# A two-layer sequence trunk: its long convolution as half-length transforms over even and odd tokens, and a new order of the first mixer

## The reference, cut to what matters

```python
def hyena_mix(u, k_hat, conv_w, conv_b, skip):
    parts = jnp.split(short_conv3(u, conv_w, conv_b), 3, axis=-1)
    z = fft_long_conv(parts[0] * parts[1], k_hat[:, 0], skip[0])
    return z * parts[2]

def fft_long_conv(z, k_hat, skip):               # k_hat = rfft of a learned filter of 2L taps
    z_hat = jnp.fft.rfft(z, n=2 * L, axis=1)
    y = jnp.fft.irfft(z_hat * k_hat, n=2 * L, axis=1)[:, :L]
    return y + z * skip

# GLA, per head and chunk of 64 tokens, forward and backward in time
att = tril(q_in @ k_in.T);  o = att @ v + q_in @ state_before;  state = decay * state + k_st.T @ v
y = concat([hyena(hy), rms_norm(o_f + o_b) * silu(g)]) @ w_out
```

## Time and profile before

| | |
|---|---|
| median of three runs | 1725.1 us |
| the profiled execution, its own time | 1726.82 us |
| its span on the core | 1725.0 us |
| TensorE busy | 1688.2 us, 98% |
| VectorE busy | 1154.5 us, 67% |
| ScalarE busy | 683.7 us, 40% |
| GpSimd busy | 72.3 us, 4% |
| bytes moved | 249.73 MB, mean 145 GB/s |

### The profile page before, as it was taken

The page is one execution under the profiler, slowest core; times in us unless marked ns, Lnnn a source line. Parts: engine busy times, 40 slices in busy tenths (PEclk is TensorE's granted clock), DMA queues, the critical chain, the costliest instruction groups (busy, mean ns, idle before and its releaser), DMA issues. The chain is left out here.

```text
span 1725.0 us, 24359 instructions
## 1 busy us (share of the span) xinstructions
PE 1688.2 (98%) x9608; PEld 1438.4 (83%) x9608; DVE 1154.5 (67%) x1791; ACT 683.7 (40%) x1058; POOL 72.3 (4%) x60
## 2 busy tenths in 40 slices
PE   7999999999999999999999999999999999989997
PEld 4788888889778679888888889888888888889997
DVE  5477949877385767677733366879466787765556
ACT  4443232225353326532222237322232267664443
POOL 1000000011000011000000020000000110100001
PEclk9999999999999999999999999999999999989998
DMA  9565546632332011555322233554466342245653
GB/s 333 222 207 173 169 157 212 211 92 74 112 116 83 26 58 73 197 187 182 112 97 94 84 139 101 197 175 154 162 216 204 92 144 77 75 142 161 205 165 110
DMA packets 86375, 249.73 MB, mean 145 GB/s; under 512 B 8740, under 2 KB 24261, under 8 KB 86262
## 3 DMA queue, kind: packets, MB, share of 16 engines
q1 hardware_dynamic: 85592, 246.25, 43.1%
q0 software_dynamic: 448, 1.51, 0.2%
q10 hardware_dynamic: 222, 0.43, 0.1%
HBM read 247.10 MB, written 1.05 MB: 144 GB/s over the span
## 5 line engine op out<-in xcount | busy, mean ns | idle before, releaser
L1872 PE MATMUL bank<-a_hi,w_hi 128*128 128x512 f32 (+1 forms) x1528 | 556.9, 364 | 7.6 <-DVE yt L1696 2.8
L1873 PE MATMUL bank<-a_hi,w_lo 128*128 128x512 f32 (+1 forms) x1528 | 555.1, 363 | 0.0
L1874 PE MATMUL bank<-a_lo,w_hi 128*128 128x512 f32 (+1 forms) x1528 | 555.1, 363 | 0.0
L1154 DVE TENSOR_TENSOR w_lo<-raw,w_hi 128x1024 fp32r<-128x1024 f32 (+1 forms) x338 | 381.6, 1129 | 177.0 <-ACT w_hi L775 170.0
L775 ACT CAST w_hi<-raw 128x1024 fp32r<-128x1024 f32 (+1 forms) x338 | 320.2, 953 | 162.5 <-DMA raw<-in_dram 155.2
L1872 PEld LDWEIGHTS bank<-a_hi,w_hi 128*128 128x128 f32 x1528 | 289.2, 189 | 55.3 <-issue 7.9
L1874 PEld LDWEIGHTS bank<-a_lo,w_hi 128*128 128x128 f32 x1528 | 289.2, 189 | 45.0
L1873 PEld LDWEIGHTS bank<-a_hi,w_lo 128*128 128x128 f32 x1528 | 289.2, 189 | 44.7
L1172 DVE SCALAR_TENSOR_TENSOR acc<-ada,scol,acc 128x1024 f32<-128x1024 f32 x189 | 234.8, 1279 | 4.7 <-DMA ada<-in_dram 2.3
L1872 PE MATMUL bank<-h_hi,w_hi 128*128 128x512 f32 (+1 forms) x638 | 230.2, 361 | 0.0
L1874 PE MATMUL bank<-h_lo,w_hi 128*128 128x512 f32 (+1 forms) x638 | 229.6, 360 | 0.0
(11 more groups left out here) (293 smaller groups left out, 1799.2 us busy)
## 6 DMA issues: line engine op xcount, KB each, us to landing
raw<-in_dram SPq DMA_DIRECT2D x229, 512.0 KB, 3.6
ada<-in_dram SPq DMA_DIRECT2D x120, 512.0 KB, 3.9
raw<-in_dram SPq DMA_DIRECT2D x64, 384.0 KB, 3.2
raw<-in_dram SPq DMA_DIRECT2D x64, 320.0 KB, 2.9
first<-in_dram SPq DMA_DIRECT2D x32, 256.0 KB, 8.0
first<-in_dram SPq DMA_DIRECT2D x8, 512.0 KB, 10.5
hz<-in_dram SPq DMA_DIRECT2D x4, 512.0 KB, 7.9
out_dram<-hz SPq DMA_DIRECT2D x8, 128.0 KB, 1.7
```

The source lines that it names most:

```text
L1154: V.tensor_tensor(lo_of(n)[:, 0:cols], raw[:, n % RING, 0:cols], hi_of(n)[:, 0:cols].bitcast(F32), ALU.subtract).then_inc(s["lo_ready"], 1)
L1872: pe.matmul(dst, w_at(0), x_at(0), start=first, stop=False, skip_group_check=shared)
L1873: pe.matmul(dst, w_at(1), x_at(0), start=False, stop=False, skip_group_check=shared)
L1874: return pe.matmul(dst, w_at(0), x_at(1), start=False, stop=last, skip_group_check=shared)
```

## The change

The transform of 512 points is replaced by one at half-step frequencies over the even and the odd tokens apart: a table of 128 tokens by 128 frequencies for each parity (`turns_tab`), of which sums and differences give both halves of the band. The filter's spectrum is made in the same way, so that the single extra frequency (L2169) goes. The forward table is rotated by half a step on the chip, from a part of the old table and two columns of sines (`half_turn`), and the table for the way back is the transposed forward one (`inverse_tab`). The transfers of the two tables in the mixer go; at the start the window comes in six transfers instead of one, and the table in four, ahead of the second group of `first`.

In the mixer the units come in a new order: after one v unit the gate's products, then the rest of v, the eight Hyena units that make `zf` with attention, keys and states between them, then the g units and the last four Hyena units, with the forward products behind g 0 and g 2 and the products back between the last Hyena units. Some copies move between ScalarE and VectorE: v, the scaling of `o_sb`, the squares' sums and the skip term are now ScalarE's.

```diff
+Z_UNITS = 2 * YC
+HY_ORDER = [(c, part) for c in range(YC) for part in range(2)] + [(c, 2) for c in range(YC)]
+DFT_AFTER = (0, 2)
+INVERSE_AFTER = ((), (0, 1), (2,), (3,))
...
-            sp.dma_start(window[:, 0:3, :], window_d[:, 0:3, :]).then_inc(s["window_in"], 16)
+            for i, part in enumerate((0, 0, 2)):
+                for b in range(2):
+                    sp.dma_start(window[b * GCH:(b + 1) * GCH, i, :], window_d[i % 2::2, part + b, :]).then_inc(s["window_in"], 16)
+            for odd in range(2):
+                for b in range(2):
+                    src = dft_d[odd::2, b, :].rearrange("p (a f) -> p a f", a=2)
+                    sp.dma_start(dft0[b * GCH:(b + 1) * GCH, odd], src[:, :, 0:P]).then_inc(s["dft0_in"], 16)
```

ScalarE at the start:

```diff
+                for kind in range(2):
+                    for odd in range(2):
+                        A.activation(dft_mix[:, odd, kind, :], dft0[:, odd, 1 - kind, :], ACT.Copy,
+                                     scale=half_turn[:, 1, odd:odd + 1]).then_inc(s["tab_scaled"], 1)
```

VectorE at the start:

```diff
+                for kind, op in enumerate((ALU.add, ALU.subtract)):
+                    rotated(kind)
+                    for odd in range(2):
+                        V.tensor_tensor(tmix[:, 2 * kind + odd, :], taps[:, odd, :], taps[:, 2 + odd, :], op)\
+                            .then_inc(s["taps_mixed"], 1)
```

TensorE at the start, in `spectrum`:

```diff
-                    for b in range(2):
-                        ins = pe.matmul(fbank(6 + i)[:], dft0[:, b, i * P:(i + 1) * P], tmix[:, (i // 2) * 2 + b, :],
-                                        start=(b == 0), stop=(b == 1))
-                    ins.then_inc(s["spectrum"], 1)
+                    pe.matmul(fbank(6 + i)[:], turns_tab[:, i % 2, i // 2, :], tmix[:, i, :], start=True, stop=True)\
+                        .then_inc(s["spectrum"], 1)
```

VectorE in the mixer:

```diff
+                def halves(w):
+                    m = mix[w]
+                    for kind in range(2):
+                        j = plan.base[("dft", w, 2 * kind)]
+                        job_ready(dve, j)
+                        dve.wait_ge(s["odd_kept"], 2 * w + kind + 3)
+                        even, odd = jbank(j)[:], m[:, 4 + kind, :]
+                        V.tensor_tensor(m[:, 2 * kind, :], even, odd, ALU.add)
+                        V.tensor_tensor(m[:, 2 * kind + 1, :], odd if kind else even, even if kind else odd, ALU.subtract)\
+                            .then_inc(s["dft_read"], 1)
...
+                root_of_squares()
+                dve.wait_ge(s["o_done"], 2)
+                split_to(plan.base[("g", 0)][0] + 4)
+                halves(0)
                 spectra(0)
+                split_to(plan.base[("g", 1)][0] + 4)
+                split_to(plan.base[("g", 2)][0] + 4)
+                halves(1)
                 spectra(1)
```

TensorE in the mixer:

```diff
+                def transform(w):
+                    if w == 0:
+                        pe.wait_ge(s["zt_read"], TC)
+                    for part in range(4):
+                        j = plan.base[("dft", w, part)]
+                        bank_read(pe, j)
+                        pe.matmul(jbank(j)[:], turns_tab[:, part % 2, part // 2, :], zt[:, 2 * w + part % 2, :],
+                                  start=True, stop=True).then_inc(s["dft"], 1)
+                def inverse(c):
+                    j = plan.base[("idft", c)]
+                    bank_read(pe, j)
+                    for w in range(2):
+                        pe.wait_ge(s["spec_out"], w + 1)
+                        for odd in range(2):
+                            for kind in range(2):
+                                at = odd * SEQ + w * P
+                                ins = pe.matmul(jbank(j)[:, at:at + P], mix[w][:, (5, 2, 7, 3)[2 * odd + kind], c * P:(c + 1) * P],
+                                                inverse_tab[:, odd, kind, :], start=(kind == 0), stop=(kind == 1))
+                    ins.then_inc(s["idft"], 1)
...
+                unit("g", 0)
+                transform(0)
+                unit("g", 1)
+                unit("g", 2)
+                transform(1)
                 pe.wait_ge(s["o_scaled"], TC)
...
+                unit("g", 3)
+                for c in range(YC):
+                    unit("hy", Z_UNITS + c)
+                    for x in INVERSE_AFTER[c]:
+                        inverse(x)
```

More of the change, by code:

```diff
@@ L432, in hybrid_trunk @@
         kst = put("kst", [P, 4, T], at=X + 48 * K)
-        state_two = [put(f"state{i}", [P, NLAT, 2, 2, P], at=X + (8 + 40 * i) * K) for i in range(2)]
+        state_two = [put(f"state{i}", [P, NLAT, 2, 2, P], at=X + (72 - 24 * i) * K) for i in range(2)]
         v = put("v", [P, TC, GH * GDV], at=X + 56 * K)
@@ new lines, in even_mixer, with middle_tap @@
+                act.wait_ge(s["w_used"], first_unit("e_v") + 4)
+                for t in range(TC):
+                    A.copy(v[:, t, :], bank[4 + t][:]).then_inc(s["v_read"], 1)
+                def middle_tap(i):
+                    c, part = HY_ORDER[i]
+                    j = plan.base[("hy", i)][1]
+                    job_ready(act, j)
+                    dst = part2[:, c, :] if part == 2 else cv[:, part, c % 2, :]
+                    A.activation(dst, jbank(j)[:], ACT.Identity, bias=pcol("conv_b", YC * part + c),
+                                 scale=pcol("conv_w", 3 * YC + YC * part + c)).then_inc(s["hy_mid"], 1)
@@ new lines, in even_mixer @@
+                for i in range(Z_UNITS):
+                    split_to(plan.base[("hy", i)][0] + 4)
+                    if HY_ORDER[i][1] == 0 and HY_ORDER[i][0] >= 2:
+                        act.wait_ge(s["zf_ready"], HY_ORDER[i][0] - 1)
+                    middle_tap(i)
+                    if i == 6:
+                        act.wait_ge(s["tab_turned"], 2)
+                        A.activation(inverse_tab[:].rearrange("p a b f -> p (a b f)"), bank[6][:], ACT.Copy, scale=2.0 / NFREQ)\
+                            .then_inc(s["tab_scaled"], 1)
+                    if i == 3:
@@ L2128, in filter_and_slot_0 @@
                 pe.matmul(fbank(0)[0:FHID, 0:SEQ], fw1[:], feats[:], start=True, stop=True).then_inc(s["filter_h"], 1)
+                for odd in range(2):
+                    ins = pe.matmul(bank[6][:, 64 + odd:65 + odd], feats[0:1, odd::2], ones[0:1, 0:1], start=True, stop=True)
+                ins.then_inc(s["tab_turned"], 1)
                 pe.wait_ge(s["silu_c"], 1)
@@ L2165, in tap_norms @@
             def tap_norms():
-                pe.wait_ge(s["spectrum_read"], 3)
-                for b in range(2):
-                    ins = pe.matmul(fbank(10)[0:1, :], dft0[:, b, SEQ:SEQ + 1], tmix[:, b, :],
-                                    start=(b == 0), stop=(b == 1))
-                ins.then_inc(s["nyquist"], 1)
                 pe.wait_ge(s["spectrum_read"], 4)
```

555 lines of the change are left out of this document (307 added, 248 removed).

## The result

| | before | after |
|---|---|---|
| median | 1725.16 us (4 runs, 1724.89 to 1727.00) | 1706.11 us (4 runs, 1704.97 to 1707.00) |
| the profiled execution's own time | 1726.82 us | 1705.41 us |
| its span | 1725.0 us | 1703.6 us |

A forecast was written before the change was run, and what follows sets the result against it. TensorE, busy 1688.2 of 1725.0 us, was taken to bound the kernel. Mixer -21.8, extra frequency -1.9 and the rest of the start 0 summed to -23.7 us; from 1725.1, near 1701, range 1696 to 1710.

The forecast's parts named there:

- VectorE late in the spectra: Rival in the mixer: VectorE falls behind TensorE, adding a few us of waits and low clock, 1707 us; chance 0.21.
- forward products: Mixer: eight products of 128x512 take the place of sixteen, saving 7.0 of 14.0 us.
- products back: Mixer: 32 matmuls stay but their columns halve, 14.2 us becomes 7.6, saving 6.6; 0 kept as the other end.
- waits gone: Mixer: TensorE's waits for `yt` (2.8 us), two unit remainders (2.8) and the spectrum (1.2) go, saving 6.8 us.
- two stretches at the lower clock: Mixer: two stretches at granted clock 0.66, behind waits of TensorE, cost 1.7 us each and go, saving 3.4 us.
- new waits in the mixer: Second Hyena unit's remainder 0.2 us, two chunk-state jobs 0.1 each, `zf` 1.1; sum 1.5 us, no clock price.
- start: Before the mixer: extra frequency gone, -1.9 us; 3.9 us less of spectrum products exchanged for waits on sums, 0 net.
- I cost it at nothing: Start: ten small transfers cost SP some 5 us of issue, but the queues have a backlog, so charged 0.
- No saving on the products back: Rival in the mixer: the products back do not get cheaper, +6.6 us, so 1708 us; chance 0.08.
- the start's full gain: Rival at the start: the 3.9 us of spectrum products are gained, so 1697 us; chance 0.09.
- no gain: Rival in the mixer: removed work returns as 23.7 us of TensorE waits on VectorE, 1725 us; chance 0.02.
- slower: Rival in the mixer: TensorE runs at half rate for long, eight units giving 1740 us, twelve 1760; chance 0.03.

The follow-up runs named there:

- the four-wide run: Changed kernel with the output projection's first four units side by side, as in the kernel before, in place of two pairs: 1711.95 us, one execution.
- the run with a later `zf`: Changed kernel with four extra VectorE products of 128x512 ahead of the last product into `zf`: 1711.07 us.
- two transfers: Changed kernel with window and table in one transfer each instead of ten, same bytes, all 128 partitions, rows in wrong places: 1704.95 us.
- sums first: Changed kernel with VectorE taking the sums of the second and following groups ahead of the spectrum's work: 1705.53 us.
- read first: Changed kernel with VectorE reading each of the first eight Hyena units' banks ahead of the next remainder instead of behind it: 1707.72 us.
- products twice: Changed kernel with every forward product and every product back issued twice: 1719.95 us.
- ScalarE's queue: Changed kernel with the ten small transfers of window and table issued from ScalarE behind its first Sin instead of from SP: 1707.62 us.
- seven transfers: Changed kernel with VectorE's sums ahead of the spectrum's work, last remainder behind `zf`, and window and table in seven transfers of 128 partitions: 1721.17 us.

## Why the prediction was right, and where it was off

The forecast was 1701 us, the result 1706.1: inside the range of 1696 to 1710, but 5 us above the point and 2 above the band of 1698 to 1704 that had most of the chances. The number is nearest to the rival with VectorE late in the spectra (1707), which is not what happened. The terms, for the profiled executions:

| term | predicted | measured |
|---|---|---|
| forward products | -7.0 | -6.8 (14.0 to 7.2) |
| products back | -6.6 | -6.6 (14.2 to 7.6) |
| transposes of the table | +0.5 | +0.6 |
| waits gone | -6.8 | -6.8 |
| two stretches at the lower clock | -3.4 | -3.4 |
| new waits in the mixer | +1.5 | +2.9 |
| start | -1.9 | -1.0 |
| sum | -23.7 | -21.1 by the terms, -21.4 by the spans and times |

**Products.** Right to 0.2 us. The end kept for the products back, no saving, was refuted, and with it what the prediction set against the change: 64 loads of 192 ns lie inside 7.6 us of products that use all 128 rows. Doubling both groups confirmed nearly all of the price on the path (13.4 of 14.1 us). The nearest row, 16 transposes of the same width, was a better guide than the length of a load.

**Waits and clock.** The sizes were right for the profiled executions; for the median it is open whether both stretches count. The reason for the largest was not: the prediction put the end of the wait for `yt` down to 11 us of other work ahead of it. That work stands behind four banks, and the four-wide run waited 3.76 us with it. The wait went because two banks suffice for a pair: the term came out right by luck. In the mixer no wait passed 1.2 us and no stretch fell below the full clock, as predicted; the run with a later `zf` had both (3.58 us, and 0.54 from 530 to 535).

**New waits.** `zf` was predicted at 1.1 and took 1.17 us; the cause, a remainder in VectorE's chain, is shown by its removal. The bank behind `halves` was called just in time and was 0.35 us late. The remainder of the second Hyena unit (0.2) was no wait. The mis-sized term is the chunk states: 0.2 us predicted, 1.3 measured. The walk counted when VectorE would be done with the bank, and left out that a job runs through it in pieces; 0.7 us of this has no named cause, and no run took it away.

**The start.** The step that failed is "I cost it at nothing", on the ten transfers. The premise was true, since the queues are full; the conclusion was not, because a full queue passes on whatever slows it. The rate fell to 279 GB/s, the fourth sums came at 51.34 instead of the predicted 50.9 us, and the first full unit 0.9 us later than before where the sum had it at the same time. With two transfers it came at 53.91, 0.7 us earlier than in the kernel before. The exchange of the 3.9 us of products for waits on sums was right in kind: in all the waits for sums are 5.4 us, of which 4.6 lie past the first group. The prediction had given 2 to 4 us in all as its sign, and was short there. The waits were avoidable, since sums first took 4.0 of them, but the weights' landing then takes over a part.

**From profile to median.** Of the 4.7 us between 1701.4 and 1706.1, the sum was 2.3 off between the profiled executions, and the other 2.4 are the offset. The forecast took 1.7 us off the profiled time to reach the median, as if the changed kernel's median would be at the lower level too. Its four runs were split between the levels, two and two, and the kernel before's seven runs beside the first experiments were mostly at the upper. Three runs at one level had looked like the whole spread. No term stood for stretches of lower clock outside the mixer, which come and go from one execution to the next.

**The rivals.** VectorE late in the spectra is out: its products start every 0.60 us from 546.47 on, and the second `halves` cost no wait. No saving on the products back, the start's full gain, no gain and slower are out by the rows above. The nearest to coming true was the price of the clock behind one wait more. (The first rival's worst case counted 36 operations, where the prediction's own count is 40; nothing rests on it.)

## What to carry to other kernels

Count a wait in a dense stretch of TensorE with what follows it: here two waits of 3.6 and 3.8 us cost 6.0 and 6.3 us. Before moving work ahead of or behind an operation on a waited-for engine, look whether that engine idles there, since work in idle time is free and out of it is not. A transfer in a full queue is not free if its form is slow (1.5 us here), and the form is read from the share of the engines beside the GB/s: a share of 1.11 with 279 GB/s came with the part-width transfers, a share of 0.13 with 50 GB/s with a pattern that two engines served. And before a difference of one or two us is given to an edit, compare the clock and the length of the stretches that the edit leaves alone: two of the runs here had 1.0 and 1.6 us there, as much as what was sought.

## What the runs showed of the hardware that was not expected

- A wait is not by itself followed by the lower clock. In the mixer it was, behind 1.99 and 2.8 us (twice each), 3.58 and 3.76. At the start, the same wait for the second sums was followed by a stretch at the lower clock in some runs and not in others, though the first two named here do the same at the start as the changed kernel, and its length does not decide: 2.28 us (read first, 0.80 and 0.86 from 30 to 40 us), 2.40 (products twice, 0.87 and 0.79) and 2.88 (ScalarE's queue, 0.66 from 35) were, 2.26 (two transfers) and 2.69 (after) were not. What tells them apart is open.
- The granted clock of the profile does not give the pace in the first 20 us. Before, matmuls of 512 columns start every 0.43 us from 18.91 to 21.47 us and every 0.23 us from 24.78, under a clock of 1.00 in both places; the first is the pace that the mixer shows at 1.2 GHz. After, it is the same up to 20.6 us, with no wait in front, so that the slow pace behind the wait of 1.82 us in the run with sums first (18.45 us) is only in part a matter of that wait. Behind the wait of 9.0 us with seven transfers (31.20 us) the matmuls from 36.91 to 39.47 start every 0.43 us, again at 1.00.
- The price of such a stretch is not fixed: 1.7 us behind the waits of before, 2.4 and 2.5 behind the longer ones. Outside the mixer, with no longer wait than in the changed kernel, it was 1.0 us (near 645 us, sums first and two transfers) and 1.6 (70 to 80 us, read first).
- A transfer pattern with an outermost size of two ran at 50 GB/s, against 367 in the same queue with two whole transfers, and held everything behind it for 15 us.
